# The recurrent block with its projections as three rounded products: weights and activations in two halves, gelu's square moved to ScalarE

## The reference, cut to what matters

```python
h = rmsnorm(x, norm_mix_g[i]) * (1.0 + sc1) + sh1       # 512 x 1024
u = h @ w_in                                            # 1024 -> 2 x 1280
xb, gb = jnp.split(u, 2, axis=-1)
gate = jax.nn.gelu(gb)
xc = causal_conv_of_4(xb, conv_w) + conv_b
r = sigmoid(blocks(xc) @ wr + br); i = sigmoid(blocks(xc) @ wi + bi)
log_a = -8.0 * r * softplus(-lam); a = exp(log_a)
b = sqrt(-expm1(2.0 * log_a)) * (i * xc)
hs = scan(a, b)                                         # h_t = a_t h_(t-1) + b_t
y = (hs * gate) @ w_out                                 # 1280 -> 1024
x = x + g1 * y
```

## Time and profile before

| | us |
|---|---|
| median of 3 runs | 3565.23 |
| the profiled execution's own span | 3564.8 |
| PE busy in it | 3350.9 (94%) |
| DVE, ACT, POOL busy | 1653.4, 1209.1, 1041.4 |
| end of the last row of the recurrent block | 285.5 |
| start of the first matmul of the stage behind it | 293.0 |

### The profile page before, as it was taken

How to read it: one execution, slowest core, us unless ns; L and a number is a source line. 1 busy time by engine, 2 the same in 40 slices (tenths; PEclk the granted TensorE clock), 3 DMA queues, 4 the chain that set the end, 5 groups by cost and what they waited for, 6 DMA issues and landing times.

```text
span 3564.8 us, 43025 instructions
## 1 busy us (share of the span) xinstructions
PE 3350.9 (94%) x17544; PEld 2485.4 (70%) x17544; DVE 1653.4 (46%) x3116; ACT 1209.1 (34%) x2188; POOL 1041.4 (29%) x906
## 2 busy tenths in 40 slices
PE   7999999888899999989899998999999998999998
PEld 3446888655688865645588856888887547848886
DVE  6744446598466666314466614122224118621223
ACT  2413323347323236125423214211113226733222
POOL 0233444551244420011255303223222022024443
PEclk9999999999999999989999999999999999999999
DMA  7424555210255541100122121111111111012222
GB/s 296 189 76 163 209 202 201 101 48 1 104 203 204 209 184 48 48 25 1 42 55 52 40 83 41 54 71 55 64 71 48 53 48 66 1 48 95 100 104 80
DMA packets 82405, 337.13 MB, mean 95 GB/s; under 512 B 46432, under 2 KB 50208, under 8 KB 57376
## 3 DMA queue, kind: packets, MB, share of 16 engines
q1 hardware_dynamic: 81344, 332.14, 25.1%
q10 hardware_dynamic: 864, 2.24, 0.2%
HBM read 326.64 MB, written 7.70 MB: 94 GB/s over the span
## 4 chain that ended last, share of the span: by engine, by line
PE 78%; DVE 11%; ACT 4%; POOL 3%; DMA 2%; issue 2%; SPq 1%; POOLq 0%; DVEq 0%; ACTq 0%
PE PSB L559 15%; PE PSB L651 14%; PE PSB L655 14%; PE PSB L652 14%; PE PSB L1237 3%; PE PSB L1259 2%; PE PSB L1246 2%; PE PSB L3087 1%; DVE SB L392 1%; DMA SB<-in_ada 1%; PE PSB L1798 1%; DVE SB L1331 1%; DVE SB L1642 1%; DVE SB L1347 1%; DVE SB L1640 1%
## 5 line engine op out<-in xcount | busy, mean ns | idle before, releaser
L655 PE MATMUL PSB<-R,WSR 128*128 128x512 f32 x2556 | 871.2, 371 | 0.0
L559 PE MATMUL PSB<-SB 128*128 128x512 f32 x1760 | 654.9, 534 | 11.7 <-ACT SB L1457 9.2
L625 POOL TENSOR_TENSOR WSR<-SB,ahead 128x1024 fp32r<-128x1024 f32 x164 | 392.8, 2395 | 672.7 <-ACT ahead L594 672.7
L559 PEld LDWEIGHTS PSB<-SB 128*128 128x128 f32 x1760 | 338.6, 193 | 325.3 <-issue 298.9
L651 PE MATMUL PSB<-R,ahead 128*128 128x512 f32 x1528 | 561.9, 368 | 0.0
L652 PE MATMUL PSB<-R,ahead 128*128 128x512 f32 x1528 | 546.0, 367 | 0.0
L655 PEld LDWEIGHTS PSB<-R,WSR 128*128 128x128 f32 x2556 | 449.1, 189 | 63.1
L625 POOL TENSOR_TENSOR WSR<-SB,ffn_weights 128x1024 fp32r<-128x1024 f32 x96 | 230.0, 2396 | 389.4 <-ACT ffn_weights L594 389.4
L651 PE MATMUL PSB<-R,ffn_weights 128*128 128x512 f32 x868 | 324.4, 374 | 8.3 <-POOL WSR L625 8.3
L651 PEld LDWEIGHTS PSB<-R,ahead 128*128 128x128 f32 x1528 | 286.9, 188 | 63.4
L652 PEld LDWEIGHTS PSB<-R,ahead 128*128 128x128 f32 x1528 | 286.9, 188 | 48.5
(11 more groups left out here) (378 smaller groups left out, 4813.6 us busy)
## 6 DMA issues: line engine op xcount, KB each, us to landing
SB<-in_w SPq DMA_DIRECT2D x95, 2048.0 KB, 8.1
SB<-in_ada SPq DMA_DIRECT2D x96, 1024.0 KB, 5.2
SB<-gate_rows SPq DMA_DIRECT2D x12, 512.0 KB, 4.0
SB<-in_rpb SPq DMA_DIRECT2D x8, 448.0 KB, 3.6
spill<-SB SPq DMA_DIRECT2D x1, 3072.0 KB, 9.6
SB<-gate_rows SPq DMA_DIRECT2D x24, 128.0 KB, 3.9
SB<-spill SPq DMA_DIRECT2D x1, 3072.0 KB, 9.9
SB<-in_x SPq DMA_DIRECT2D x8, 256.0 KB, 6.9
```

The lines of the kernel that those rows point to most:

```text
L559: ins = e.mm(banks[ring[(g + c) % len(ring)]][0:m, 0:n], t[:, 0:m], xs[k][:, lo:lo + n], k == 0, k == nkt - 1)
L625: e.tt(lr, t, hf, ALU.subtract).then_inc(*G.up(("lo", j)))
L655: ins = e.mm(b[:, 0:n], wl, xh[:, lo:lo + n], False, last)
```

## The change

It does the projections of the recurrent block, but not its gates, as three rounded products.

- h is made as a pair (high, low): DVE writes the scaled tile to one of three PSUM banks, ACT adds the shift and rounds, DVE subtracts to get the low part.
- Weight groups of 8 tiles: `front` has four buffers for high parts, `back` two, `last` (for `a_out`) four. ACT's and POOL's lists get one operation for each of the 30 groups, at the places shown.
- y's high part is a copy by ACT, its low part a subtraction by POOL.
- gelu's square is taken by ACT out of PSUM with the factor under it; DVE makes the argument in one operation, and POOL's three operations go. u is kept in M, the scans' results in XCV's place (HS = XCV), and gated_x waits for the gates of its block.
- The first two rows of `a_out` go side by side, k outermost.
- Six modulation halves are still loaded early, one of them to another place; the context's load waits for the front's group 7.

```diff
-    stat("a_out", 8, 10)
+    plan.extend(("a_out", k, m) for k in range(10) for m in range(2))
+    stat("a_out", 6, 10, 2)
-            H, SQ = tiles(8, S), tiles(2, S)
+            H, SQ = pairs(8, S), tiles(2, S)
-            XCV, HS, M = tiles(10, S), tiles(10, S), tiles(10, S)
+            XCV, M = tiles(10, S), tiles(10, S)
+            HS = XCV
...
+            front = HalvesInPlace(st, of_in[0:80], WS + XS)
+            back = HalvesInPlace(st, of_in[80:160], WS, 10)
+            last = HalvesInPlace(st, [t for t in W.plan if t and t[0] == "a_out"],
+                                 [...rounded_tiles... for i in range(4)], 20)
+            T = banks[4:7]
...  pe: rows 0 to 3
+                            e.wait_ge(*st.at("hi", j))
                             e.wait_ge(*st.at("h", k))
+                            e.mm(b, wh, xh, k == 0, False)
+                            e.mm(b, wh, xl, False, False)
+                            e.wait_ge(*st.at("lo", j))
+                            ins = e.mm(b, wl, xh, False, k == 7)
-                g = linear(e, st, g, ring, "a_in", range(10, 20), 8, H, LAT, lambda k, lo: [])
+                g = linear3(e, st, g, ring, back, "a_in", range(10, 20), range(8), H, LAT, lambda x, lo: [])
+                g = turn3(e, st, g, ring, last, "a_out", (0, 1), range(10), YH, LAT, ready)
+                linear3(e, st, g, ring, last, "a_out", range(2, 8), range(10), YH, LAT, ready)
...  act
                 for f in range(8):
                     e.wait_ge(*st.at("scaled", f))
-                    e.act(H[f], H[f], ACT.Identity, bias=sh[:, f:f + 1]).then_inc(*A.up(("h", f)))
+                    e.act(H[f][1], T[f % 3], ACT.Identity, bias=sh[:, f:f + 1]).then_inc(*A.up(("h_hi", f)))
+                    if f < 4:
+                        front.act(e, A, f)
...
                     e.act(XB[mt][:, 3:3 + S], banks[ring[mt % 6]], ACT.Copy).then_inc(*A.up(("bank", mt), ("xb", mt)))
+                    front.act(e, A, mt + 4)
+                e.wait_ge(*st.at("group_used", 8))
+                back.act(e, A, 0)
...
                     e.act(AA[f], AA[f], ACT.Exp, scale=c4[:, f:f + 1], bias=c4[:, f:f + 1]).then_inc(*A.up(("a", f)))
+                    if f == 7:
+                        e.wait_ge(*st.at("group_used", 9))
+                        back.act(e, A, 1)
...
                 for mt in rows:
                     e.wait_ge(*st.at("mm", g))
                     e.wait_ge(*st.at("scan", mt))
-                    e.act(XCV[mt], banks[ring[g % 6]], ACT.Copy).then_inc(*A.up(("bank", g), ("u", mt)))
+                    e.act(M[mt], banks[ring[g % 6]], ACT.Copy).then_inc(*A.up(("u", mt)))
+                    e.act(AA[mt], banks[ring[g % 6]], ACT.Square, scale=0.044715 ** 0.5).then_inc(*A.up(("bank", g), ("u_square", mt)))
+                    back.act(e, A, mt + 2)
+                    if mt:
+                        rounded_y(mt - 1)
                     e.wait_ge(*st.at("gelu_arg", mt))
                     e.act(AA[mt], AA[mt], ACT.Tanh, scale=0.7978845608028654).then_inc(*A.up(("gelu_tanh", mt)))
+                    if mt == 8:
+                        e.wait_ge(*st.at("half", 2 * len(fill.jobs) - 1))
+                        for j in range(3):
+                            last.act(e, A, j)
...  dve
+                def rest(f):
+                    v.wait_ge(*st.at("h_hi", f))
+                    v.stt(H[f][2], T[f % 3], sh[:, f:f + 1], H[f][0], ALU.add, ALU.subtract).then_inc(*D.up(("h", f)))
...
                     v.wait_ge(*st.at("gate", 2 * f + 1))
+                    v.wait_ge(*st.at("mm", 10 + 4 * (f // 2) + 3))
                     v.stt(HS[f], M[f], 1.0, XCV[f], ALU.add, ALU.mult).then_inc(*D.up(("gated_x", f)))
...  dve, behind all ten scans
+                v.wait_ge(*st.at("u_square", 0))
+                v.stt(AA[0], AA[0], 1.0, M[0], ALU.add, ALU.mult).then_inc(*D.up(("gelu_arg", 0)))
                 for mt in rows:
+                    if mt < 9:
+                        v.wait_ge(*st.at("u_square", mt + 1))
+                        v.stt(AA[mt + 1], AA[mt + 1], 1.0, M[mt + 1], ALU.add, ALU.mult).then_inc(*D.up(("gelu_arg", mt + 1)))
                     v.wait_ge(*st.at("gelu_tanh", mt))
-                    v.stt(AA[mt], AA[mt], 1.0, XCV[mt], ALU.add, ALU.mult).then_inc(*D.up())
+                    v.stt(AA[mt], AA[mt], 1.0, M[mt], ALU.add, ALU.mult).then_inc(*D.up())
...  pool: groups 0 to 3, the pads, groups 4 to 9, back's group 0, then
                     e.tt(SQ[f % 2], AA[f], AA[f], ALU.mult).then_inc(*G.up(("a_square", f)))
+                    if f == 7:
+                        back.pool(e, G, 1)
+                def rest_of_y(k):
+                    e.wait_ge(*st.at("y_hi", k))
+                    e.tt(YH[k][2], HS[k], high_of_y[k][0], ALU.subtract).then_inc(*G.up(("y", k)))
                 for mt in rows:
-                    e.tt(t, u, u, ALU.mult).then_inc(*G.up())
-                    e.ts(t, t, 0.044715, 1.0, ALU.mult, ALU.add).then_inc(*G.up())
-                    e.tt(t, t, u, ALU.mult).then_inc(*G.up(("gelu_arg", mt)))
+                    back.pool(e, G, mt + 2)
+                    if mt:
+                        rest_of_y(mt - 1)
+                    if mt == 8:
+                        for j in range(3):
+                            last.pool(e, G, j)
+                rest_of_y(9)
+                for j in range(3, 10):
+                    last.pool(e, G, j)
```

More of the change, by code:

```diff
@@ L310 @@
 LOG_EXP = "natural_log_exp_and_others"
[L311 removed]
+SPLIT = ("a_in", "a_out", "b_in", "b_out", "f1_0", "f2_0", "f1_1", "f2_1", "g_0", "u_0", "d_0", "g_1", "u_1", "d_1")
 class Weights:
@@ L592, in act, with take @@
                     if j >= len(self.bufs):
[L593 to L605, removed]
+                        e.wait_ge(*self.st.at("group_used", self.e0 + j - len(self.bufs)))
+                    e.act(hr, t, ACT.Copy).then_inc(*A.up(("hi", self.e0 + j)))
+            def take(self, name, k, m, n=1):
                 i = self.of[name, k, m]
@@ L784, in pe @@
                     for mt in range(4):
+                        b = banks[ring[mt]]
                         for k in range(4 * half, 4 * half + 4):
-                            t, landed = W.tile("a_in", k, mt)
-                            e.wait_ge(*landed)
+                            wh, wl, j, used = front.take("a_in", k, mt)
+                            _, xh, xl = H[k]
+                            e.wait_ge(*st.at("hi", j))
                             e.wait_ge(*st.at("h", k))
-                            ins = e.mm(banks[ring[mt]], t, H[k], k == 0, k == 7)
+                            e.mm(b, wh, xh, k == 0, False)
+                            e.mm(b, wh, xl, False, False)
+                            e.wait_ge(*st.at("lo", j))
+                            ins = e.mm(b, wl, xh, False, k == 7)
                             if k == 7:
-                                ins.then_inc(*P.up(("mm", mt), *W.done("a_in", k, mt)))
-                g = linear(e, st, 4, ring, "a_in", rows[4:], 8, H, LAT, lambda k, lo: [])
+                                ins.then_inc(*P.up(("mm", mt), *used))
+                g = linear3(e, st, 4, ring, front, "a_in", rows[4:], range(8), H, LAT, lambda x, lo: [])
                 for f, name in gates:
@@ L821, in act, with rounded_y @@
                 e.load(conds[0], d_cond[0].partition_broadcast(128)).then_inc(cond_landed[0], 16)
+                def rounded_y(k):
+                    e.wait_ge(*st.at("gated", k))
+                    e.act(YH[k][1], HS[k], ACT.Copy).then_inc(*A.up(("y_hi", k)))
                 condition(e, 0)
@@ L874, in act @@
                         e.wait_ge(*st.at("squares", mt - 2))
-                    e.act(H[0] if mt == 0 else H[1 + mt % 2], X[mt], ACT.Square).then_inc(*A.up(("sq", mt)))
+                    e.act(Q[0] if mt == 0 else Q[1 + mt % 2], X[mt], ACT.Square).then_inc(*A.up(("sq", mt)))
                     if mt >= 6:
@@ L940, in dve @@
                     if mt:
-                        add_square(v, D, st, H[0], H[1 + (mt - 1) % 2], mt - 1)
+                        add_square(v, D, st, Q[0], Q[1 + (mt - 1) % 2], mt - 1)
             def pool(e):
+                for j in range(4):
+                    front.pool(e, G, j)
                 for mt in rows:
+                    e.wait_ge(*st.at("half", 0))
                     e.memset(XB[mt][:, 0:3], 0.0).then_inc(*G.up(("pad", mt)))
+                for j in range(4, 10):
+                    front.pool(e, G, j)
+                back.pool(e, G, 0)
                 for f in rows:
```

57 lines of the change are left out of this document (39 added, 18 removed).

## The result

The changed kernel takes 3604.76 us (3597.47 to 3607.31, 4 runs) where the kernel before takes 3564.96 us (3555.05 to 3566.61, 4 runs): a ratio of 1.0106, with a 95% interval of 1.0093 to 1.012. It is 39.8 us slower. The forecast was 3601 us, in a range of 3575 to 3622. The profiled execution of the changed kernel spans 3605.5 us.

The account below looks back on a forecast made before the run. PE paced the stage before; after the change the path was taken to run over DVE and ACT. Terms 20.3 - 5.8 + 34.2 - 13.3 made the stage 35.4 us later, so 3601 us, range 3575 to 3622.

Parts of the forecast that it names:

- 1. *h.: Head of the stage, up to h's last tile: 8.6 us later, from ACT's list order, two holds and added DVE operations.
- 2. *Convolutions.: Convolutions on DVE: of the weight groups subtracted there, some five and a half hold DVE, 11.2 us; sum so far 19.8.
- 3. *Gates to first scan.: Last convolution's end to first scan's end: 55.7 us, plus 3.5 for back's group 1, less 3.0 for a load; sum 20.3.
- 4. *Scans.: First to last scan's end: 18.9 us instead of 24.7, without POOL's gelu operations between; sum 14.5.
- 5. *Gelu.: Last scan to last gated row: 64.2 us instead of 30.0, in turns of 6.5 us; 34.2 more, sum 48.7.
- 6. *`a_out`.: Last gated row to the stage's end: 48.1 us instead of 61.4, 13.3 less; stage ends 35.4 us later.
- keeps its length: Behind the stage: everything starts from the same state and takes as long as before, so nothing is added there.
- Few or short holds: POOL's subtractions hardly hold DVE: 3570 us with no holds, 3585 if only gelu's turns escape; 3572 to 3590, chance 0.17.
- Table loads: In gelu, Square can't share tanh's table, so each turn loads twice, 26 us in all: 3622 us; chance 0.09.
- PE stays the bound and the time falls: DVE's chain is covered, last gated row ends before about 225 us, 43.6 us come off PE: 3530 us; faster, chance 0.06.
- signs named ahead: Trace after: operations lengthened beside subtractions, PE idle before two back rows, 6.5 us turns, last gated row near 272 us.

## Why the prediction was right, and where it was not

The mechanism, the place and the size held: the time lies with DVE and ACT, PE waits, the stage ends 34.6 us later where 35.4 were forecast. By its steps:

1. *h.* The last tile came 7.9 us later (DVE ends its low part at 53.63 + 1.59 = 55.2; before, ACT ended it at 44.63 + 2.70 = 47.3), forecast 8.6; both holds fell on modulation operations as said. The step failed in what it left out: it ended at h and gave the convolutions the same delay, though softplus stands between them on DVE. Its 10-column operations took four holds, 8.5 us. A 0.17 us operation is held for as long as one of 1.27 us.
2. *Convolutions.* Forecast 11.2 us for five and a half holds among seven groups; 5.9 came, from three. The other four are those that met softplus. So all seven met DVE, and of steps 1 and 2 together 19.8 us were forecast and 21.5 came: the total was near because a hold costs the same wherever it falls. ACT's waits of 21.0 and 6.2 us for the panels were not foreseen either, and PE's front rows ended near 113 us, not 101; neither shows on the path, since DVE was busy throughout (54.94 of 56 us).
3. *Gates to first scan.* 57.0 us, forecast 56.2 (55.7 + 3.5 - 3.0). Of the 3.0 us that I took back for the gate panel's load 1.5 were there: a modulation half still came 2.79 us late, where it had been 4.29. The additions then cost 2.8 of the 3.5 us.
4. *Scans.* 18.6 us, forecast 18.9, one scan held (3.25 instead of 1.22).
5. *Gelu.* 62.5 us, forecast 64.2; turn 6.29, forecast 6.5, through the same operations. The overlap of neighbours' ends (0.1 us each) makes the difference.
6. *`a_out`.* 46.8 us from last gated row to the end, forecast 48.1.

The sum fits partly by luck: step 1 was 7.0 us short (15.6 came up to the first convolution) and step 2 5.3 us too long, and steps 5 and 6 were too long by 1.7 and 1.3. The 5 us behind the stage were no part of it ("keeps its length" was the step that failed there), and they are why 3604.8 stands above 3601.

The rivals. Few or short holds: the kernel without subtractions gives what it would have been, 3577.71 us with a stage 7.2 us longer than before (forecast 5); the changed kernel has the holds. That rival's sum held a wrong term: it took back 4.2 us for the gates, which no row gives, and the run shows 0.9 us more than before from the last convolution to the first scan (56.65 and 55.71), while gelu took 23.1 us more than before, not 25.0. Table loads: refuted. Square runs between two tanhs in 0.58 us, with no load between them. The Trainium skill (ScalarE: Activation LUTs, Table sets: the hidden batching unit) names relu, copy, identity and abs as the functions in every set; the trace shows that square shares at least tanh's and, by the very first square, the square root's. PE stays the bound and the time falls: it decides at the last gated row, which had to end before 225 us and ended at 273; the kernel with `a_out` alone shows this mechanism where it holds, 223.6 us and 3551.46. The reason given against it, that no row has a turn under 3.1 us, was no limit: the kernel with gelu alone has one of 2.36 us. Of the signs named ahead, all were seen but one: the convolution's held operations were 2.8 us beside a subtraction in three places only, and softplus in four.

## What to carry to other kernels

Faster products pay only where PE is the bound and stays it: of the 43.6 us that the three rounded products take off PE here, nearly all of the 14.5 of `a_out` were had (13.7 in the whole time), because the work that they add on ACT and POOL lies under rows that stay slow, and the other 29 were not in any arrangement run, because there they add to the chain that is the bound next. When POOL is given large two-input operations, count the operations of VectorE that start while one runs, the shortest included; each is worth one whole hold. And look in each hand-written list at what stands behind the waiting instruction: a weight group behind a tanh cost PE 12 us in one kernel and 10 in another.

## What the runs showed of the hardware

- A VectorE operation of 10 columns on SBUF took 2.2 to 2.3 us instead of 0.17 beside a 1024-column subtraction of GpSimd, with one tensor input (L304) as with two (L302). It isn't the operation's own traffic that sets the price.
- A memset of 1024 columns on GpSimd (0.95 us) held the 10-column operation with one tensor input for 0.6 us (L304: 0.74 instead of 0.17), and not the one with two (L302 kept its 0.17, and so did the larger ones their lengths: three convolution operations beside it took 2.33 us as ever).
- GpSimd's subtraction is slowed as well: 2.35 to 2.40 us alone, 2.56 beside one held product, 5.42 us for two beside the convolution, 6.72 for two beside the modulation; four beside the 10-column operations were not slowed (4.75 and 4.76 for two).
- In the changed kernel, waits of PE of 15.6 and 12.4 us were each followed by some 4 to 5 us at a mean granted clock of 0.61. One stretch of unchanged work took 19.4, 20.0 or 22.9 us, with the granted clock at 1.00, 0.91 and 0.78 and the other engines' work the same.
